# Four small edits to a one-core decoder step: filler transposes, turned state-space outputs taken by two engines, an index list moved inside a product, and the expert order read place by place

## The reference, cut to what matters

```python
h = rms_norm(x, norm1_g);  z = h @ w_in                    # split into u, q, three K/V sets, gates
y, state = s5_scan(u, h0, ...)                             # complex diagonal state space, 32 groups of 16
zg = gelu(y);  glu = zg * sigmoid(zg @ w_glu + b_glu)      # (rows, 512)
o_nsa = nsa_attention(q, ...)                              # compressed + selected + window attention
merged = sigmoid(g_a) * (glu @ w_ssm_out) + sigmoid(g_b) * (o_nsa @ w_nsa_out)
x = x + merged @ w_o
x = x + hier_moe(rms_norm(x, norm2_g))                     # top-1 of 4 groups, top-2 of 4 experts in it
x = x + sigmoid(x @ w_ple_gate) * (p @ w_ple);  out = rms_norm(x, final_norm_g)
```

## Time and profile before

| | |
|---|---|
| median of 3 runs | 842.35 us (841.59 to 847.88) |
| the profiled execution's own time | 841.85 us |
| its span from first to last instruction | 840.1 us |
| TensorE busy | 801.1 us, 95% of the span |
| VectorE, ScalarE, GpSimd busy | 42%, 23%, 17% |
| TensorE's granted clock, mean | 0.989 of full |
| moved by the transfer engines | 137.54 MB |

### The profile page before, as it was taken

The page is one execution under the profiler, slowest core; times in us unless marked ns, Lnnn a source line. Parts: engine busy times, 40 slices in busy tenths (PEclk is TensorE's granted clock), DMA queues, the critical chain, the costliest instruction groups (busy, mean ns, idle before and its releaser), DMA issues. The chain is left out here.

```text
span 840.1 us, 13591 instructions
## 1 busy us (share of the span) xinstructions
PE 801.1 (95%) x5079; PEld 521.9 (62%) x5079; DVE 352.8 (42%) x957; ACT 194.3 (23%) x462; POOL 139.7 (17%) x151
## 2 busy tenths in 40 slices
PE   7999999999999899889999999999889999999995
PEld 5465677877778689555566774445765655654441
DVE  3189902655551423766634471125721111124433
ACT  3010201211011253655423100044011111122222
POOL 3049100500003011334400100012110111004000
PEclk9999999999999899999999999999999999999998
DMA  9530494622302587600020485015799999977011
GB/s 329 129 120 0 129 267 160 121 22 79 142 29 67 121 176 217 178 1 2 1 114 2 118 319 197 1 51 166 295 388 366 391 418 418 352 286 263 28 51 37
DMA packets 81509, 137.54 MB, mean 164 GB/s; under 512 B 33958, under 2 KB 57578, under 8 KB 77234
## 3 DMA queue, kind: packets, MB, share of 16 engines
q1 hardware_dynamic: 64636, 110.17, 40.3%
q0 software_dynamic: 3872, 13.90, 4.8%
q10 hardware_dynamic: 12942, 12.64, 4.5%
HBM read 117.08 MB, written 21.72 MB: 165 GB/s over the span
## 5 line engine op out<-in xcount | busy, mean ns | idle before, releaser
L1138 PE MATMUL ps<-hT,w_slot 128*128 128x288 f32 x640 | 155.7, 406 | 0.0
L1138 PEld LDWEIGHTS ps<-hT,w_slot 128*128 128x128 f32 x640 | 121.4, 190 | 34.1 <-issue 0.6
L1138 PE MATMUL ps<-w_slot,hT 128*128 128x512 f32 (+1 forms) x320 | 127.1, 555 | 1.7 <-DMA w_slot<-in_w_in 1.4
L1138 PEld LDWEIGHTS ps<-w_slot,hT 128*128 128x128 f32 x320 | 60.0, 190 | 62.6 <-issue 42.4
L1138 PE MATMUL ps<-w_slot,merged 128*128 128x512 f32 x128 | 56.0, 594 | 1.1 <-DVE merged L2090 1.1
L2553 DVE SCALAR_TENSOR_TENSOR th<-th,ps 128x256 f32<-128x256 f32 x13 | 5.5, 421 | 112.3 <-ACT th L2017 112.3
L1623 PE MATMUL ps<-wgu,hT 128*32 128x256 f32 x480 | 42.6, 380 | 0.0
L1138 PEld LDWEIGHTS ps<-w_slot,merged 128*128 128x128 f32 x128 | 23.9, 190 | 29.9 <-issue 28.2
L1611 PE MATMUL ps<-w_slot,hT 128*128 128x256 f32 x160 | 35.8, 382 | 0.0
L1611 PEld LDWEIGHTS ps<-w_slot,hT 128*128 128x128 f32 x160 | 30.1, 190 | 7.7 <-issue 3.8
L1138 PE MATMUL ps<-qg,w_slot 128*128 128x288 f32 x128 | 33.7, 408 | 0.0
(11 more groups left out here) (444 smaller groups left out, 1250.3 us busy)
## 6 DMA issues: line engine op xcount, KB each, us to landing
merged<-in_w_exp_down SPq DMA_DIRECT2D x11, 1024.0 KB, 9.7
w_slot<-in_w_in SPq DMA_DIRECT2D x8, 1024.0 KB, 6.9
wgu<-in_w_exp_gate SPq DMA_DIRECT2D x8, 1024.0 KB, 14.5
wgu<-in_w_exp_up SPq DMA_DIRECT2D x8, 1024.0 KB, 16.5
w_slot<-in_w_exp_gate SPq DMA_DIRECT2D x8, 1024.0 KB, 8.4
w_slot<-in_w_exp_up SPq DMA_DIRECT2D x8, 1024.0 KB, 11.5
expert_rows<-onsaT ACTq DMA_DIRECT2D x13, 512.0 KB, 8.2
w_slot<-in_w_exp_down SPq DMA_DIRECT2D x5, 1024.0 KB
```

The lines of the kernel that those rows point to most:

```text
L1138: ins = pe.matmul(out, a, b, start=(n == 0), stop=(n == len(pairs) - 1))
```

## The change

Four parts:

1. **Entry fillers.** Ten more filler transposes after the transposes of tile 0 in the entry.
2. **State-space outputs.** The jobs `zg` stand ahead of `fin` on TensorE and in the plan. Those of even t are taken by VectorE, those of odd t by ScalarE. Twelve filler transposes stand between the last `y` job and the wait for the GELU. TensorE and VectorE wait for the last two copies, of either engine. ScalarE takes `fin` after its four copies.
3. **List of the slots.** `list_by_slot` of the expert loop moves from behind `gate_up` of pass 0 to inside its second half, ahead of that half's product k = 3.
4. **Order of the loads.** The down weights of experts 0 and 1 are no longer issued ahead of the wait for `order_made`, but behind it, and the values of `order_i` are read each just ahead of the first load that needs it; the last twelve are read after the load of the fourth gate and up weights.

```diff
@@ make_plan
+    for t in range(CH):
+        p.add(("zg", t), "act" if t % 2 else "dve")
     p.add(("fin",), "act")
-    for t in range(CH):
-        p.add(("zg", t), "dve")
@@ SP
             sp.wait_ge(pe_done, PLAN.done(("wo", NT - 2, 1)))
-            for u in range(2):
-                load_down(u, u)
             sp.wait_ge(order_made, 1)
-            at_place = [0, 1] + [sp.value_load(order_i[0:1, i:i + 1], min_val=0, max_val=NE - 1) for i in range(2, NE)]
+            at_place = {0: 0, 1: 1}
...
+            def read_place(l):
+                i = LOADED[l]
+                at_place[i] = sp.value_load(order_i[0:1, i:i + 1], min_val=0, max_val=NE - 1)
+
+            load_down(0, 0)
+            read_place(2)
             load_gate_up(2, expert(2))
+            load_down(1, 1)
             load_down(2, expert(2))
+            read_place(3)
             load_gate_up(3, expert(3))
+            for l in range(4, NE):
+                read_place(l)
@@ TensorE, entry
                         finish(ins)
+                    if t == 0:
+                        keep_busy(10)
@@ TensorE, state space
+            keep_busy(12)
+            pe.wait_ge(y_gelu, 8)
+            for t in range(CH):
+                o = begin(("zg", t))
+                for b in range(4):
+                    ins = pe.transpose(o[:, NCH * b:NCH * b + NCH], uc[:, t, P * b:P * b + P], ident[0:NCH, 0:NCH])
+                finish(ins)
             o = begin(("fin",))
...
-            pe.wait_ge(y_gelu, 8)
-            for t in range(CH):
...
+            pe.wait_ge(*emptied(("zg", CH - 2)))
             pe.wait_ge(*emptied(("zg", CH - 1)))
@@ TensorE, experts
-            def gate_up(j, n, u, between=None):
+            def gate_up(j, n, u, between=None, late=None):
...
+                        if w and k == 3 and late:
+                            late()
...
-                gate_up(j, 0, 0, lambda: turn_rows(j, 1, 1, 0))
-                list_by_slot(ps[:, RING], j * 4 + 2, ids, NPASS).then_inc(list_done, 1)
+                gate_up(j, 0, 0, lambda: turn_rows(j, 1, 1, 0),
+                        lambda: list_by_slot(ps[:, RING], j * 4 + 2, ids, NPASS).then_inc(list_done, 1))
@@ ScalarE
+            for t in range(1, CH, 2):
+                o = take(("zg", t))
+                empty(act.activation(zgT.rearrange("p k (c t) -> p k c t", t=CH)[:, :, :, t],
+                                     o[:, 0:4 * NCH].rearrange("p (k c) -> p k c", k=4), ACT.Copy))
             o = take(("fin",))
@@ VectorE
-            for t in range(CH):
+            for t in range(0, CH, 2):
                 o = take(("zg", t))
...
+            dve.wait_ge(*emptied(("zg", CH - 2)))
             dve.wait_ge(*emptied(("zg", CH - 1)))
```

## The result

The changed kernel takes 838.33 us (median of 8 runs, 835.98 to 839.15), the kernel before on the same chips 845.12 us (8 runs, 841.59 to 848.94). The ratio is 0.991, 95% interval 0.989 to 0.993: 0.9% faster, where 0.75% was predicted. The profiled execution took 836.80 us with a span of 835.0 us and a mean clock of 0.994.

What follows compares the result with a forecast made beforehand. It took TensorE, busy nearly the whole span, as the bound, with transfers a close second limit in the expert stage: 841.85 - 3.55 - 2.15 - 1.4 + 1.0 = 835.75 us, given as 836.0 on the median's scale, range 833.0 to 840.5.

Steps and rivals of the forecast that it cites:

- transfers set the pace: Rival, late expert passes: pass 2's 3.55 us are waited for again at the down weights; 838.3 us, chance 0.18.
- Outputs by two engines: State-space outputs: copies shared by VectorE and ScalarE bring the unit's first product 2.1 us earlier.
- The clock behind it: Gated unit's products behind the outputs: clock holds at 1.00, 2.0 us gained, of which 1.5 count.
- The cap by the write of `fin`: Stage after the unit: waits for SP's write landing at 303.5, so outputs and clock give 3.55 us, not 4.1.
- The list: Experts, pass 2: list ahead of ten matrix instructions, so the gather leaves and lands earlier, 2.15 us gained.
- the clock, 1.4 us: Behind the gather of pass 2: no half clock after the shorter wait, 1.4 us gained, bounds 0 and 1.4.
- Order of the loads, +1.0 us: Expert stage: later down weights lengthen TensorE's two waits for them by 1.0 us together, bounds -1.5 and +3.5.
- the slower rival: First transposes of the experts: pass 0's gather is caught in the weights, TensorE loses 5.0 us; 846.2 us, chance 0.06.
- all gained: Rival, whole change: all 7.1 us gained and the down weights' waits of 1.5 us vanish; 833.25 us, chance 0.18.
- Entry fillers, 0: Kernel entry: ten fillers fit TensorE's 1.41 us wait for weights and change nothing, bounds -0.1 and +0.2 us.

Runs made afterwards that it cites:

- w_fin_early: Changed kernel with SP's two writes of `fin` issued ahead of the compression weights in its queue; 838.72 us, ratio 0.993.
- p_list: Kernel before with part 3 alone, the list of the slots inside the second half of pass 0; 839.05 us, ratio 0.994.
- w_downs_early: Changed kernel with the two down weights issued ahead of `order_made` again, the reads still in place; 837.06 us, ratio 0.990.
- x_both_attn: Changed kernel with `fin` written ahead of compression weights, down weights ahead of the order, and twelve more masking products in the attention; 835.49 us, ratio 0.990.

## Why the prediction was right, and where it was not

It said 836.0 us and 833.0 to 840.5; 838.33 lies in it. That is on another footing than it seems: the kernel before measured 845.12 us over eight runs, not 842.35. Its profile, from which the sum was worked out, had a mean clock of 0.989, where 31 timed runs of the same kernel had 0.986; that is worth up to about 2 us. In microseconds the result so fell where the prediction had put "transfers set the pace" (838 to 840), which did not happen. The changes are -0.75% and -0.89%, and that they agree so well is in part luck: the two places that the sum is about gave 2.4 + 3.05 = 5.4 us of its 6.1, and 1.65 us more came in late stages, which it took as unchanged. By its own steps:

**Outputs by two engines, 2.1 us.** Measured 1.74. The mis-sized term is ScalarE's copy, taken as 0.50 us from the tanh; the four took 2.31 us, the last one from 286.26 to 286.99, and 0.73 to 0.77 each, just over its upper bound of 0.7. The fillers cost nothing, as said.

**The clock behind it, 2.0 us.** 17.65 - 15.76 = 1.89. It held in eight of eight profiles with two engines and fillers. The Trainium skill (TensorE: Matmul & The Clock Gate, Part 4: PE-mode transpose) says that transposes do not count as busy for the clock gate; the fillers are transposes, and without them the clock fell in one of two profiles, with them in none of eight. The trace still speaks against the rule, if with few cases; what speaks most plainly is the rise from 0.50 to 1.00 within transposes alone.

**The cap by the write of `fin`.** Right as a mechanism for the changed kernel, and w_fin_early shows it; in four of the seven profiles with two engines and the write in its old place it did not bind. The failed sentence is "nothing of the change moves it" and the landing at 303.5: it landed at 305.1, with the issue 0.9 us later (half of it because the last `y` job was 0.46 us later) and 4.6 us to landing in place of 3.9. The stage gained 2.38 us in place of 3.55. In the profiles with SP's old order the write lands 21.4 to 23.2 us behind the last `y` job; what in SP's queue sets that is open.

**The list, 2.15 us, and the clock, 1.4 us.** The gather left 2.17 us sooner; no slow clock at pass 2 in ten of ten profiles with the early list, one in four of four with the late one. p_list gives 3.71 us for the predicted 3.55.

**Order of the loads, +1.0 us.** The size was near and the place was wrong. The prediction put it at the waits for down weights, which did not grow (0.9 us). It falls on the gather of pass 2, which I had kept at "the same 9.24 us". There late down weights cost 1.6 us and part 4 as a whole about 1.0; the changed kernel has 3.05 us of p_list's 3.71. The gather of pass 0, which I did examine, took 5.26 us within its room, and the 1.24 us wait stood: the slower rival did not happen.

**Transfers set the pace** did not happen: of 3.05 us at the first down product all are there at the expert rows, and 0.85 more. By the number, "all gained" (-8.6) came nearest of the rivals: against the predicted 6.1 us the repeating stages gave -2.4 - 3.05 - 0.85 - 0.8 = -7.1. Its mechanism is not shown: the changed kernel waited for down weights 0.9 us in one profile and not at all in the other. The last two terms lie within what other profiles of the same stages scatter (130.3 to 132.7 and 91.8 to 93.1 us), so I claim no cause for them.

**Entry fillers, 0.** They cost nothing where they stand, as said, but ten instructions more behind a stall 143 us later cost 0.55 us, over the bound of +0.2: the step looked only at the wait beside them. Timed alone they are 1.001 (0.999 to 1.003).

**What the sum left out.** It took every stage outside the change as constant, without saying so. They moved by up to 4 us from one execution to the next.

## What to carry to other kernels

When one profile of each kernel is compared, cut both at the same points and subtract the stages that the change cannot reach before reading a gain of a few microseconds. When a late wait is shortened, read which transfer is issued last in the queue that the next stage waits for: an output write behind weight loads took back 1.2 us in both profiles of the changed kernel, and moving it ahead cost nothing. When loads are delayed into a full stretch, look not only at those who wait for the loads but at the small gather that shares the engines with them. When TensorE stops with no releaser in a dense run of short products, look for a packet of the instruction queue ahead of its end (next section).

## What the runs showed of the hardware

**A stall with no releaser that ends behind a packet of instructions.** TensorE between 145 and 154 us, in the changed kernel and, below, in w_downs_early:

```profile
145.42 3.27 PE L1233 MATMUL ps<-ident,vn 128*128 128x128 f32 x28 [1.37 <-DVE xg L2240]
148.63 2.01 PE L1242 MATMUL ps<-gm,bbar 64*32 64x128 f32 x126
153.48 0.38 PE L1242 MATMUL ps<-gm,bbar 64*32 64x128 f32 x2 [2.84 <-issue]
```

```profile
145.46 4.94 PE L1233 MATMUL ps<-ident,vn 128*128 128x128 f32 x28 [1.37 <-DVE xg L2240]
150.33 2.01 PE L1242 MATMUL ps<-gm,bbar 64*32 64x128 f32 x126
152.85 0.38 PE L1242 MATMUL ps<-gm,bbar 64*32 64x128 f32 x2 [0.51 <-issue]
```

Where the clock was 0.50 at 145 us (five of fourteen profiles, the kernel before among them), the stall was 0.9 us or less, in x_both_attn none; in the nine others it was 2.6 to 3.3 us. A full clock ahead of it only waits longer. In seven of the nine the clock fell during the long stall or right behind it, and the last `y` job ended at 283.1 to 285.0 us; in the other seven profiles at 280.6 to 281.9.

That the stall keeps its place in the count of TensorE's instructions when ten are added ahead of it speaks for the loading of code, and so do the transfers. In each of the fourteen profiles one packet of the instruction queue q8, 16 KB, starts between 149.5 and 152.5 us, ahead of the stall's end, and takes 1.1 us. The whole queue on the page, and, below, in the changed kernel from 150.6 to 153.5 us:

```profile
q8 instruction: 41, 0.67, 0.3%
```

```profile
q8 instruction: 1, 0.02, 2.3%
```

The packet is done at 152.02 us in the kernel before and at 152.07 in the changed kernel, and TensorE goes on at 153.57 and 153.48. In the thirteen profiles with a stall its end varies from 152.85 to 155.03 us and always lies 1.35 to 1.58 us behind the end of that packet. In x_both_attn the packet was done at 150.60, earlier than in any other, and there was no stall. The 41 packets are one for about 250 of the 10,202 products and weight loads that the page counts for TensorE, and here TensorE did 126 products and as many weight loads in 2.0 us. The simplest reading is that TensorE waits for its own next instructions. It is not shown by an experiment: no run moved the packet on purpose.

**The same gap takes the clock down in some executions only.** The waits of 0.72, 0.51 and 1.08 us near 375 us stand in all profiles but the last, where the third is 0.41. At or behind them the clock fell in eight of fourteen, for 3.4 us (attention about 287 us) or 6.8 (about 288), and not in six (about 285.4). So a fall in one profile shows neither that a change brought it nor that one cured it. At the outputs (four of four against none of eight) and at pass 2 (four of four against none of ten) there are enough of them.

**An indirect gather of the same list** took 5.3 to 10.0 us. Its first packet came 1.8 us after the issue in three profiles, those with early down weights and the order read in place, and 4.1 to 4.2 us after it in the other eleven.
